# Expert rows placed among the matmuls by planned landings, tokens turned before the queries, state increments before the second outputs

## What is computed

```python
def peer(h, wq, keys, u, v):
    xb = h.reshape(-1, PEER_BLOCK, D_MODEL)
    def one(xs):
        q = (xs @ wq).reshape(PEER_BLOCK, PEER_HEADS, 2, PEER_HALF)
        s1 = jnp.einsum('nhd,hkd->nhk', q[:, :, 0], keys[0]).astype(F32)
        s2 = jnp.einsum('nhd,hkd->nhk', q[:, :, 1], keys[1]).astype(F32)
        t1, i1 = lax.top_k(s1, PEER_TOPK)
        t2, i2 = lax.top_k(s2, PEER_TOPK)
...
        top, j = lax.top_k(cand, PEER_TOPK)
        eid = jnp.take_along_axis(cid, j, axis=-1)
        g = jax.nn.softmax(top, axis=-1).astype(xs.dtype)
        a = jax.nn.gelu(jnp.einsum('nd,nhjd->nhj', xs, u[eid]), approximate=False)
        return jnp.einsum('nhj,nhjd->nd', g * a, v[eid])
...
    for i in range(DEPTH):
...
        h = rmsnorm(x_lat, norm1_g[i]) * (1.0 + sc1) + sh1
        hc = rmsnorm(x_ctx, norm1_g[i]) * (1.0 + csc1) + csh1
        y, yc = token_mixer(h, hc, w_in[i], ...)
        x_lat = x_lat + g1 * y
        h2 = rmsnorm(x_lat, norm2_g[i]) * (1.0 + sc2) + sh2
        x_lat = x_lat + g2 * peer(h2, peer_wq[i], peer_keys[i], peer_u[i], peer_v[i])
        if with_ctx:
            x_ctx = x_ctx + cg1 * yc
            hc2 = rmsnorm(x_ctx, norm2_g[i]) * (1.0 + csc2) + csh2
            x_ctx = x_ctx + cg2 * peer(hc2, ...)
    return rmsnorm(x_lat, final_norm_g)
...
    def step(S, inp):
...
        att = jnp.where(mask, jnp.einsum('bhtd,bhsd->bhts', qe, ke), 0.0)
        o = jnp.einsum('bhts,bhsv->bhtv', att, vc) + jnp.einsum('bhtd,bhdv->bhtv', qe, S)
        S = jnp.exp(b_last[:, :, 0, :])[..., None] * S + jnp.einsum('bhsd,bhsv->bhdv', kd, vc)
        return S, o
```

## Time and profile before

| | us |
|---|---|
| median of 3 runs | 3924.62 |
| lowest, highest | 3921.03, 3938.82 |
| profiled execution: time | 3918.83 |
| its span | 3916.8 |

### The profile page before, as it was taken

How to read it: one execution, slowest core, us unless ns; L and a number is a source line. 1 busy time by engine, 2 the same in 40 slices (tenths; PEclk the granted TensorE clock), 3 DMA queues, 4 the chain that set the end, 5 groups by cost and what they waited for, 6 DMA issues and landing times.

```text
span 3916.8 us, 42711 instructions
## 1 busy us (share of the span) xinstructions
PE 2971.8 (76%) x16338; PEld 1845.1 (47%) x16338; DVE 1745.4 (45%) x4348; ACT 1099.5 (28%) x3076; POOL 826.4 (21%) x772
## 2 busy tenths in 40 slices
PE   7888997887889998676775655588899975555555
PEld 5677886554556665253431111166788751111111
DVE  1313012355465555535576666513211136666664
ACT  3112101332454442313432322231320113222322
POOL 0000000111222332312234434300000013343342
PEclk8899998888999998788887676688999988777777
DMA  7544433475878998767789999930224259999997
GB/s 300 210 173 155 152 139 135 179 279 215 312 295 347 402 412 350 308 236 307 313 345 395 381 394 395 392 135 33 102 97 152 77 207 386 393 394 382 388 394 285
DMA packets 151107, 1071.77 MB, mean 274 GB/s; under 512 B 16564, under 2 KB 18228, under 8 KB 22520
## 3 DMA queue, kind: packets, MB, share of 16 engines
q0 software_dynamic: 110592, 805.36, 51.1%
q1 hardware_dynamic: 40312, 263.69, 17.9%
HBM read 1067.93 MB, written 1.05 MB: 273 GB/s over the span
## 4 chain that ended last, share of the span: by engine, by line
PE 53%; DMA 26%; DVE 9%; ACT 7%; issue 3%; POOL 2%; DVEq 0%; ACTq 0%; SPq 0%; POOLq 0%
PE bank L302 40%; DMA ring<-in_experts,eid 23%; PE bank L316 10%; DVE ring L1198 4%; DMA weights<-in_quads 3%; POOL ring L1586 2%; PE bank L391 1%; DVE state L1370 1%; ACT topk_work L770 1%; ACT topk_work L763 1%; ACT hT L825 1%; ACT L760 1%; PE bank L329 1%; DVE topk_work L1168 0%; ACT topk_work L760 0%
## 5 line engine op out<-in xcount | busy, mean ns | idle before, releaser
L316 PE MATMUL bank<-ring,topk_work 64*64 64x512 f32 x6144 | 1013.4, 789 | 637.4 <-ACT topk_work L770 626.5
L1586 POOL DMA_INDIRECT ring<-in_experts,eid x768 | 826.2, 1076 | 3052.9 <-PE bank L316 1441.1
L1198 DVE CUSTOM_DVE_ANT_0 ring<-ring,h2tok 128x1024 f32<-128x1024 f32 x768 | 939.5, 1224 | 769.7 <-DMA ring<-in_experts,eid 768.0
L316 PEld LDWEIGHTS bank<-ring,topk_work 64*64 64x64 f32 x6144 | 242.4, 163 | 1326.9 <-ACT topk_work L770 1002.0
L302 PE MATMUL bank<-hT,weights 128*128 128x256 f32 (+1 forms) x1968 | 479.9, 404 | 93.4 <-ACT hT L825 52.1
L302 PEld LDWEIGHTS bank<-hT,weights 128*128 128x128 f32 (+1 forms) x1968 | 382.1, 197 | 205.0 <-ACT hT L825 54.3
L760 ACT ACTIVATE topk_work<-topk_work 128x2 f32<-128x2 f32 x384 | 78.0, 203 | 1323.4 <-DVE topk_work L1198 1291.6
L770 ACT ACTIVATE topk_work<-const,topk_work 128x64 f32<-128x64 f32 x768 | 225.7, 341 | 48.7 <-PE bank L316 47.9
L302 PE MATMUL bank<-hT,ring 128*128 128x256 f32 (+1 forms) x864 | 197.2, 388 | 9.6 <-ACT hT L825 4.6
L763 ACT ACTIVATE topk_work<-topk_work 128x1 f32<-128x1 f32 x768 | 184.6, 287 | 12.6
L302 PEld LDWEIGHTS bank<-hT,ring 128*128 128x128 f32 (+1 forms) x864 | 163.8, 190 | 39.1 <-issue 9.6
(11 more groups left out here) (205 smaller groups left out, 3005.0 us busy)
## 6 DMA issues: line engine op xcount, KB each, us to landing
weights<-in_quads SPq DMA_DIRECT2D x137, 1024.0 KB
ring<-in_quads SPq DMA_DIRECT2D x98, 1024.0 KB, 4.9
ring<-in_experts,eid POOLq DMA_INDIRECT x768
weights<-in_quads SPq DMA_DIRECT2D x7, 768.0 KB
ring<-in_quads SPq DMA_DIRECT2D x5, 768.0 KB, 6.0
weights<-in_quads SPq DMA_DIRECT2D x12, 256.0 KB
xT<-in_xT SPq DMA_DIRECT2D x1, 2048.0 KB, 11.3
out<-hT SPq DMA_DIRECT2D x1, 1024.0 KB, 4.5
```

The lines of the kernel that those rows point to most:

```text
L316: x = nc.tensor.matmul(acc[g][out, :], diag[mine, J % 4, :], ring[mine, J % RING, D + h * 512:D + (h + 1) * 512], start=first, stop=J % TI ...
L1198: v.tensor_tensor_reduce(row, row, h2tok[:, u // UNITS % 2, :], 1.0, 0.0, ALU.mult, ALU.add, dots[:, u % 2, j:j + 1]).then_inc(S["dot_done ...
L1586: pool.indirect_dma_start(ring[:, J % RING, :], None, d["experts"], bass.IndirectOffsetOnAxis(eid[:, u % 2, j:j + 1], 0)).then_inc(gathere ...
```

## The change

A planner takes the pace's place. While PE's code is written out, `Plan` keeps a clock: each matmul adds its columns' time at full speed, each row 0.95 us, each load and each gather is served by one line of transfers at 2.6 us with 2.0 us of latency. `breathe` emits a pair when its planned landing plus 6.0 us (`LAG`) is reached, with an optional `hole`, a time in which PE is going to wait anyway. DVE and ACT take up a pair ahead of a bank when PE already has it, or when its planned landing is before the planned time at which the bank is full (ACT 3.0 us later), with bounds on how far ahead (`reached`). `h2_out` of tile 0 stands ahead of the queries on all engines, pairs may be placed among the queries up to the unit whose scores stand (`rows_of_queries`), in passes 0 and 3 too, and pass 1 goes on to pair 131. In the gated attention the increments of both halves stand ahead of the second outputs, with `breathe(2.0)` between; on DVE the scaling is split in two, `carry` is called by half and the outputs are copied between the halves (`sum_out`).

```diff
--- before.py
+++ after.py
...
 FIXED, EXTRA = 2, 4
-PACE = (0.0, 4.6, 3.0, 0.0)
-AHEAD_DVE, AHEAD_ACT = 4, 3
+
+
+PER_LOAD, LANDS, LAG = 2.6, 2.0, 6.0
+LEAD_CHOICE = 14.0
+DIAG_LAG = 3.0
 
...
+class Plan:
+
+    def __init__(self):
+        self.now, self.free = 0.0, 0.0
+        self.asked, self.loads, self.rows, self.taken = [], [], [], 0
+
+    def serve(self):
+        for t, landings in sorted(self.asked, key=lambda x: x[0]):
+            self.free = max(self.free, t) + PER_LOAD
+            landings.append(self.free + LANDS)
+        self.asked = []
+
+    def load(self):
+        self.asked.append((self.now, self.loads))
+
+    def gather(self):
+        self.asked.append((self.now, self.rows))
+
+    def take_load(self):
+        if len(self.loads) <= self.taken:
+            self.serve()
+        self.now = max(self.now, self.loads[self.taken])
+        self.taken += 1
+
+    def row(self, J):
+        if len(self.rows) <= J:
+            self.serve()
+        return self.rows[J]
+
+    def first_rows(self):
+        self.serve()
+        for _ in range(RING):
+            self.asked.append((self.now + LEAD_CHOICE, self.rows))
+
+
 MOD_FIRST = [(0, q) for q in range(4)]
 MOD_LATER = [(0, q) for q in range(4, 12)] + [(n, q) for n in range(1, DEPTH) for q in range(12)]
...
+        def tile_end(k):
+
+            return (k + 1) * TILE_PAIRS + 4
+
+        def rows_beside(p):
+
+            return 0 if p.beside is None else first_pair(p.beside + 1) - (UNIT_PAIRS if p.full else 0)
+
+        def rows_of_queries(g, q):
+
+            return first_pair(g) + (2 * q + 1 if q < 3 else UNITS) * UNIT_PAIRS
+
+        def reached(n, now, deep):
+
+            if n % TILE_PAIRS == 0:
+                deep = 1
+            return placed.get(n - deep, (0, 0.0))[0] <= now
...
             def emit(n):
-                placed_now[n] = len(job_log)
+                landing = plan.row(2 * n + 1)
+                placed_now[n] = (len(job_log), landing)
+                plan.now = max(plan.now, landing + LAG)
                 row_pair(n)
-                if n % GROUP_PAIRS == TILE_PAIRS + 1:
-                    tile_sum(2 * (n // GROUP_PAIRS))
+                if n % TILE_PAIRS == 1 and n // TILE_PAIRS in (1, 2, 3, 5):
+                    tile_sum(n // TILE_PAIRS - 1)
+                for J in (2 * n, 2 * n + 1):
+                    plan.now += 0.95
+                    if not 2 * GROUP_ROWS - RING <= J < 2 * GROUP_ROWS:
+                        plan.gather()
                 cur["next"] = n + 1
 
-            def breathe():
-
-                while cur["next"] < cur["limit"] and cur["work"] >= cur["pace"]:
-                    cur["work"] -= cur["pace"]
+            def breathe(hole=0.0):
+
+                end = plan.now + hole
+                while cur["next"] < cur["limit"] and plan.row(2 * cur["next"] + 1) + LAG <= plan.now + hole / 2:
                     emit(cur["next"])
+                plan.now = max(plan.now, end)
 
...
                     dd, t = units[u]
                     order = (0, 1) if dd == 0 else (1, 0)
+                    halves = [slice(cc * CHUNK, cc * CHUNK + CHUNK) for cc in order]
+
+                    def of_state(m):
+                        for h in range(GLA_H):
+                            x = mm(ob[h // 2][halves[m], (h % 2) * DV:(h % 2) * DV + DV], gla_buf(u, GQ)[:, h, halves[m]],
+                                   state[:, dd, h, :], False, m == 1, skip_group_check=True)
+                            if m == 1 and h % 2:
+                                full(x, "o", n, u, h // 2)
+
                     if p.full:
                         pe.wait_ge(*at("gla_att", n, u))
                         ob = [job("o", n, u, g) for g in range(2)]
                         for h in range(GLA_H):
                             mm(ob[h // 2][:, (h % 2) * DV:(h % 2) * DV + DV], gla_buf(u, GA)[:, h, :],
                                Btok[:, t, h * DV:h * DV + DV], h % 2 == 0, False, skip_group_check=True)
+                        if u >= 2:
+                            pe.wait_ge(*at("evicted", "s", n, u - 2, 1, 1))
+                        else:
+                            pe.wait_ge(*at("state0", n, dd))
+                        of_state(0)
                     pe.wait_ge(*at("evicted", "kdt", n, u))
-                    for m, cc in enumerate(order):
-                        half = slice(cc * CHUNK, cc * CHUNK + CHUNK)
-                        if p.full:
-                            if m:
-                                pe.wait_ge(*at("evicted", "s", n, u, 0, 1))
-                            elif u >= 2:
-                                pe.wait_ge(*at("evicted", "s", n, u - 2, 1, 1))
-                            else:
-                                pe.wait_ge(*at("state0", n, dd))
-                            for h in range(GLA_H):
-                                x = mm(ob[h // 2][half, (h % 2) * DV:(h % 2) * DV + DV], gla_buf(u, GQ)[:, h, half],
-                                       state[:, dd, h, :], False, m == 1, skip_group_check=True)
-                                if m == 1 and h % 2:
-                                    full(x, "o", n, u, h // 2)
+                    for m in range(2):
                         for g in range(2):
                             b = job("s", n, u, m, g)
                             for h in (2 * g, 2 * g + 1):
-                                x = mm(b[:, (h % 2) * DV:(h % 2) * DV + DV], gla_buf(u, GD)[half, h, :],
-                                       Btok[half, t, h * DV:h * DV + DV], True, True)
+                                x = mm(b[:, (h % 2) * DV:(h % 2) * DV + DV], gla_buf(u, GD)[halves[m], h, :],
+                                       Btok[halves[m], t, h * DV:h * DV + DV], True, True)
                             full(x, "s", n, u, m, g)
+                    if p.full:
+                        breathe(2.0)
+                        pe.wait_ge(*at("evicted", "s", n, u, 0, 1))
+                        of_state(1)
 
...
                 for u in range(len(units) + 1):
                     if u < len(units):
+                        breathe(3.0)
                         intra(u)
-                        breathe()
                     if u + 1 < len(units):
...
+            def queries(p):
+                n, i, g = p.n, p.i, p.group
+                square_sums("norm2", n, DC)
+                breathe(8.0)
+                for k in range(DC):
+                    pe.wait_ge(*at("h", "norm2", n, k))
+                if g == 1:
+
+                    rows_until(tile_end(0))
+                turn_h2(g, 0)
+                for q in range(8):
+                    w = quad(i, "wq", q, k=DC)
+                    project(g, "pq", w, pair_of(q), HT, DC)
+                    if q == 1:
+
+                        rows_until(cur["limit"])
+                    if q % 2:
+                        w = quad(i, "keys", q // 2, k=1)
+                        for t in range(2):
+                            key_scores(g, w, t, q // 2)
+                        if q == 1 and 2 * g * UNITS in LEADS:
+                            plan.first_rows()
+                        cur["limit"] = rows_of_queries(g, q // 2)
+                cur["q"] = None
+                if g == 1:
+
+                    rows_until(tile_end(1))
+
             pe.wait_ge(const_landed, 32)
...
             def rows_before(*key):
 
-                now = job_no.get(key, 0)
-                while (cur["next"] < cur["limit"] and cur["next"] in placed and placed[cur["next"]] - AHEAD_DVE <= now
-                       and placed.get(cur["next"] - 3, 0) <= now):
-                    rows_until(cur["next"] + 1)
+                now, when = job_no.get(key, 0), full_at.get(key, 0.0)
+                while cur["next"] < cur["limit"] and cur["next"] in placed:
+                    n = cur["next"]
+                    deep = 2 if n % TILE_PAIRS == 3 else 3
+                    if placed[n][0] > now and not (placed[n][1] <= when and reached(n, now, deep)):
+                        break
+                    rows_until(n + 1)
 
...
```

217 lines of the change are left out of this document (111 added, 106 removed).

## The result

The changed kernel takes 3766.83 us, the median of 4 runs (3760.31 to 3774.84); in the same comparison the kernel before takes 3922.82 us. The profiled execution took 3774.84 us (its span is 3772.8), the highest of the four, so the two profiles differ by 144 us and not by 156.

A forecast was written before the change was run, and what follows sets the result against it. It took DMA transfers to bound row-only stages, PE the merge of pass 1, and neither to be full in the stretches changed. Terms (a) to (i) summed to -73.8 from 3918.8, giving 3845.0 profiled, 3851 us median; range 3795 to 3910.

The forecast's parts named there:

- (a): Gated attention of passes 0 and 3: shorter waits for state and output bank, -6 us each, -12 together.
- (d): Gated attention of pass 1: state waits and slower matmuls behind them, 40.1 us, shrink by -27; bounds -10 and -40.
- (b): Pass 0's queries: three inserted pairs cost +5.8 us and a delayed weight load +3.2, sum +9.0.
- (i): Pass 3's queries and the tail: three pairs moved from the row stage into the queries, -7.1 us; bounds -10 and +2.
- (e): Norm before pass 1's queries: two pairs stand in PE's 9.76 us wait, -3.9 us; 0 if their rows were late.
- (f): Pass 1's first four projections and the block of pairs up to 119: 103.7 us becomes 113.2, +9.5.
- (g): Rest of pass 1's queries: 12 pairs instead of 8, 108.2 us becomes 95, -13; bounds -25 and 0.
- (h): Pass 2: 124 pairs instead of 128 at 5.37 us each, -21.5 us; bounds allow -20 or +15 from idle DMA.
- Deeper gain: Rival: (d) gives all 40, (g) reaches PE's floor, half of pass 2's idle DMA returns; 3806 us, chance 0.20.
- The slower one: Rival: planned landings too early, so 135 pairs beside matmuls block in-order engines; 3959 us at 0.8 us more each, chance 0.07.

The follow-up runs named there:

- at the pace: Kernels whose rows go out at the kernel before's pace, not the planner's; the kernel after with only that changed: 3758.36 us, ratio 0.9574.
- the old look-ahead: Kernel after, but DVE and ACT take up pairs by the old rule (PE has them within its next 4 and 3 jobs): 3764.65 us, ratio 0.958.
- lag 12: Kernel after with LAG 12.0 instead of 6.0, so a pair is placed 6 us later: 3830.46 us, ratio 0.9747.
- the planner alone: Kernel after with increments in their old place and no new group's pair among the queries; tokens still turned ahead: 3895.53 us, ratio 0.9935.

## Why the prediction was right and wrong

What failed is the size of the waits. Terms (a) and (d) priced each wait of the gated attention at its own length, term (b) charged pairs and a later load that cost next to nothing, and some 23 us of pass 1 had no term at all. By the profiles 144 us were gained for 73.8 forecast, 70 more. Of these, 24.2 lie in (a), 10.1 in (b), 36.6 in pass 1 up to its queries (9.4 of them in (d)) and 9.3 in (i); pass 2 gave 9.9 less than forecast and pass 1's queries 0.3 less. Terms (b) to (i) rest on where the planner put the pairs, which the order told.

**Right in the sum, in part by luck: (e), (f), (g).** Pass 1's queries with their norm changed by -7.1 against -7.4, but each part is off by some: from the norm to the first query -3.1 for -3.9, the stretch to pair 119 +5.3 for +9.5 (109.0 us, forecast 113.2), the rest -9.3 for -13 (98.9 us, forecast 95, at DMA share 0.86). In (e) the number came about another way. The second pair in the norm did wait for its row, 7.14 us, the case in which the prediction gives the term 0; what went instead is a wait of 7.19 us of PE for ACT in the norm, which had no term. The load waits of (g) are 7.31 and 1.63 us, 8.9 in all (9.4 forecast, 9.3 before).

The Trainium skill, "DMA: Bandwidth & Descriptors", section "Issuing engines are not separate DMA queues", says that transfers started by any engine run on the same 16 DMA engines and interleave, and the prediction worked out from it that loads come late beside gathers. This trace has one load wait that is longer beside gathers, 7.31 us where 3.28 stood, but their sum did not grow, and the stretch took 98.9 us, not 82.

**Wrong: (a), the size.** -6 was forecast for each of passes 0 and 3; measured -19.7 and -16.5. The gated attention, windows of pass 3 in before and then in after, the whole stage and the stretch behind the first unit's last wait:

```profile
2641.10:2725.90 84.80, 67.25 (x304) 51.71 (x304) 34.69 (x65) 12.01 (x25) 0.00 (x0) 0.90 0.10 34
2671.80:2677.60 5.80, 5.77 (x29) 5.18 (x29) 2.65 (x5) 1.16 (x3) 0.00 (x0) 0.71 0.00 0
...
2530.60:2602.20 71.60, 61.78 (x305) 48.20 (x305) 34.42 (x64) 12.00 (x25) 0.00 (x0) 0.90 0.12 41
2558.20:2562.40 4.20, 4.15 (x29) 3.69 (x29) 3.70 (x8) 1.16 (x3) 0.00 (x0) 1.00 0.00 0
```

PE's idle time falls by 7.7 us, close to the 6.7 that I worked out, and its busy time by 5.5. Four times the second half's increments beside the first's make 4.1 of that (4 x 1.02). The rest is about what one stretch shows: the 29 records behind the first unit take 5.77 us at a granted clock of 0.71, behind a wait of 1.66 us, and 4.15 us at 1.00, behind one of 0.56 (1.00 is the upper of the clock's two levels, 2.4 GHz; 0.71 is a mean over both). Another 3.3 us come in the stage behind it. In pass 0 the stage goes from 95.7 to 76.4 us, idle time again by 7.6 and busy time by 11.7, at a clock of 0.96 for 0.88; some 3 us of this are spread, since the same stage with the old increments takes 92.5 to 92.7 us in four other kernels. I took the bounds, 0 to -8, from waits alone, as if the duration of a record were fixed.

**Wrong: (d), on the low side of its true size.** The mechanism was right: the state waits fell to 1.3 us (forecast below 15) and the clock rose to 0.89 (above 0.85). The gated attention of pass 1 went from 144.1 to 111.6 us with two pairs more in it, -36.4 with their 3.9 taken out, for -27. I left one DVE pair per unit in the wait, 12.8 us in all; of that, 6.2 us are there, as the wait for the masking. The bound of -40 held. The runs at the pace show what the term consists of: the new order of the increments brings 11 us there (144.1 to 132.8 us), the place for pairs behind them 27 (to 106.1).

**Not in the sum: the rest of pass 1.** Up to its queries it lost 36.6 us more than forecast. 9.4 of them are (d). 3.9 are two pairs that I counted in this block and that stand behind the norm. 14.0 are in the output projection (54.2 to 38.2 us, one pair fewer), where a wait of 11.3 us for DVE's merge output went. Of the last 9.3, 7.2 lie between the gated attention and the end of the latent attention (216.3 to 209.1 us, 25 pairs in both), all of it idle time. The wait of 11.3 us is 8.2 to 11.0 us in the other kernels at the pace and the old look-ahead, 6.0 with the planner and the old look-ahead, 4.0 at lag 12, and 0 in the kernel after and with the planner alone. The planner's kernels have 29 to 31 pairs in the merge for 36. Between the kernel after and the one with the old look-ahead only the look-ahead differs, so that takes part of the wait; that the fewer pairs take the rest is argued and not shown. These pairs stand in the queries instead, which take 227.8 us for the 188.5 of the same kernel at the pace: what the planner gains ahead of the queries it gives back in them.

**Wrong: (b).** Pass 0's queries changed by -1.1, not +9.0. I charged the three pairs 5.8 us and a delayed load 3.2. The longest load wait is 8.37 us, but it was 7.16 before and is 8.17 in the kernel without pairs among the queries: it belongs to the group's first six gathers, which all these kernels have. The six gathers that follow the pairs delayed nothing, since the last load's wait fell from 3.00 to 0.57. And the pairs stand in waits that PE had anyway. The block takes 98.2 to 103.3 us in the kernels without pairs in it and 100.0 to 104.7 in those with three, so they cost some 2 us, less than executions differ.

**(h) and (i): the pairs.** Four pairs fewer in pass 2 brought 11.6 us for 21.5; at the pace they bring 13.8 and 18.2. Three fewer after pass 3 brought 16.4 for 7.1. The queries there cost 2.9 us more (99.9 to 102.8, up to the turned tokens), not 9, as in (b): there too the last load's wait fell, from 3.26 to 0.76. The start of the row stage, up to the end of pair 261, went from 31.5 us with six pairs to 9.5 with three, 5.9 more than 3 x 5.37: the waits of 5.45 and 5.97 us, which I quoted and didn't price, went. Waits of 3.72 and 3.55 us stand right behind that point instead, and the rest of the stage takes 2.6 us more. Here the word "transfer" was wrong as well: 5.37 us a pair contained the edge of the units, and with it gone a pair costs 5.11.

**Which rival came.** Deeper gain was the direction (3806), and its reason, that fewer waits also speed up what follows, is borne out in (a). But of its three items only (d) came near (36.4 of 40); (g) stayed 16 us above PE's floor and pass 2 gave less than forecast. It was still 39 us too high. The slower one was real as a mechanism, at a lag of 2 instead of 6.

**Why half was missed.** The parts don't add in one way only. Taken out of the kernel after, the increments and the place are worth 61 us where my terms (a) and (d) held 39, and the rows in the queries 47 where the other terms held 35. Put into the kernel before at its old pace, the same two are worth 82 and 88, and 164 together, the whole gain without the planner. Either way I priced every wait at its own length and every pair at its count. What stays open is why the planner's kernels without rows in the queries are 27 us faster than those at the pace; I have the blocks in which they gain and lose, not each wait.

## What to carry to other kernels

Where an in-order engine waits for another's update, put independent work between the request and the wait, and a slot where filler can go. The new order alone was worth 58 us here, the slot (with ACT's take-up of rows ahead of it) another 29. Where the wait goes, what stands behind it may run at a higher granted clock, so a wait can be worth more than its length. A DMA share of 0.94 isn't full: look at who ends the idle time of the engine that issues. Before a planner is credited, run the kernel with the old rule and the other parts kept.

## What the runs showed of the hardware

16 matmuls whose operands stand on 64 partitions, 64x256 in fp32, take 3.72 us if all use the same half, 2.96 if eight with one half follow eight with the other, and 2.00 if they alternate. The 64 matmuls by the state took 510 and 513 ns each behind waits, at a granted clock of 0.81 in the stage, and 385 ns almost without them, at 0.89. Behind a group's first six gathers the third projection of pass 0 waited 8.17 and 8.37 us for its load (without and with pairs among the queries), the other projections at most 2.94. In a stage of rows alone the DMA reached a share of 0.99 and 404 GB/s.
